# A hybrid decoder trunk on one core: another order of PE's and VectorE's work between the attention stage and the expert gathers

## What is computed

```python
x = x + (ga * ya + gb * yb) @ w_out                     # ya: state-space branch, yb: latent attention
x = x + peer(rmsnorm(x, norm_ffn), peer_wq, peer_keys, peer_u, peer_v)

def peer(h):                                            # 8 heads, 128 keys per half, top 16
    q = (h @ wq).reshape(blk, 8, 256)
    s1, s2 = q[..., :128] @ keys[:, 0], q[..., 128:] @ keys[:, 1]
    sc1, i1 = top_k(s1, 16); sc2, i2 = top_k(s2, 16)
    cand = sc1[..., :, None] + sc2[..., None, :]        # 16 x 16 sums
    sc, sel = top_k(cand, 16); idx = cidx[sel]          # 16 of 16,384 experts
    act = gelu(u[idx] . h)
    return sum(softmax(sc) * act * v[idx])
```

## Time and profile before

| | us |
|---|---|
| median of 3 runs | 2117.23 |
| lowest and highest | 2110.43, 2120.0 |
| the profiled execution | 2117.6 |
| its span | 2116.1 |
| PE busy in it | 1670.0 (79%) |
| VectorE busy | 1447.7 (68%) |
| ScalarE busy | 489.1 (23%) |
| bytes read | 735.70 MB |

### The profile page before, as it was taken

How to read it: one execution, slowest core, us unless ns; L and a number is a source line. 1 busy time by engine, 2 the same in 40 slices (tenths; PEclk the granted TensorE clock), 3 DMA queues, 4 the chain that set the end, 5 groups by cost and what they waited for, 6 DMA issues and landing times. The chain is left out here.

```text
span 2116.1 us, 30101 instructions
## 1 busy us (share of the span) xinstructions
PE 1670.0 (79%) x10874; PEld 842.1 (40%) x10874; DVE 1447.7 (68%) x3666; ACT 489.1 (23%) x1413; POOL 667.8 (32%) x614
## 2 busy tenths in 40 slices
PE   7999999877777666666789999997777866666666
PEld 6887677433333111111168786773332421111111
DVE  3557533778778878877726575347877878887786
ACT  2246211211121221111223553122121112111112
POOL 0011000444554454444300110004454444444442
PEclk9999999877897676665799999999787876666658
DMA  5458895999999999999854688969999999999997
GB/s 205 157 204 305 300 389 229 387 370 420 416 421 421 404 416 420 421 415 414 366 181 150 218 318 297 387 240 408 404 421 420 416 420 402 421 421 420 416 413 304
DMA packets 135936, 749.11 MB, mean 354 GB/s; under 512 B 16611, under 2 KB 17100, under 8 KB 57298
## 3 DMA queue, kind: packets, MB, share of 16 engines
q0 software_dynamic: 84640, 588.54, 68.2%
q1 hardware_dynamic: 51138, 158.55, 20.6%
HBM read 735.70 MB, written 11.52 MB: 353 GB/s over the span
## 5 line engine op out<-in xcount | busy, mean ns | idle before, releaser
L1221 PE MATMUL ps<-arena 64*64 64x512 f32 x4096 | 753.2, 836 | 384.0 <-DVE arena L1841 381.7
L2463 POOL DMA_INDIRECT arena<-in_peer_uv,arena x528 | 619.9, 1174 | 792.2 <-PE ps L1221 642.7
L1832 DVE CUSTOM_DVE_ANT_0 arena<-arena,h 128x1024 f32<-128x1024 f32 x512 | 627.3, 1225 | 241.3 <-DMA arena<-in_peer_uv,arena 235.4
L1221 PEld LDWEIGHTS ps<-arena 64*64 64x64 f32 x4096 | 141.1, 166 | 938.6 <-DVE arena L1841 889.7
L573 PE MATMUL ps<-ht_tok,wring 128*128 128x264 f32 (+1 forms) x1536 | 362.9, 395 | 4.5 <-DMA wring<-in_w_in 3.1
L2204 ACT ACTIVATE arena<-arena 128x1 f32<-128x1 f32 x528 | 105.4, 203 | 975.1 <-DVE arena L1832 974.0
L573 PEld LDWEIGHTS ps<-ht_tok,wring 128*128 128x128 f32 x1536 | 292.8, 194 | 75.6 <-issue 19.9
L1841 DVE TENSOR_SCALAR arena<-consts,arena 128x64 f32<-128x64 f32 (+1 forms) x528 | 164.6, 312 | 25.2 <-ACT arena L2204 24.6
L573 PE MATMUL ps<-arena,wring 128*128 128x264 f32 x256 | 64.1, 393 | 2.7 <-DVE arena L1536 2.7
L573 PE MATMUL ps<-arena,gate 128*128 128x256 f32 x256 | 59.0, 382 | 0.0
L2440 POOL DMA_DIRECT2D nrow<-in_norm_ffn x2 | 1.1, 536 | 174.2 <-PE ps L925 174.2
(11 more groups left out here) (374 smaller groups left out, 1791.3 us busy)
## 6 DMA issues: line engine op xcount, KB each, us to landing
arena<-in_pages SPq DMA_DIRECT2D x256, 272.0 KB, 6.1
wring<-in_w_in SPq DMA_DIRECT2D x36, 1024.0 KB, 5.0
arena<-in_peer_uv,arena POOLq DMA_INDIRECT x528, 12.8
h<-in_state_ssm POOLq DMA_DIRECT2D x16, 512.0 KB, 6.1
out<-h POOLq DMA_DIRECT2D x16, 512.0 KB, 6.3
wring<-in_w_ssm_proj SPq DMA_DIRECT2D x8, 1024.0 KB, 10.8
arena<-in_w_out SPq DMA_DIRECT2D x8, 1024.0 KB, 9.4
wring<-in_peer_wq SPq DMA_DIRECT2D x8, 1024.0 KB, 9.7
```

The lines of the kernel that those rows point to most:

```text
L1221: last = pe.matmul(ps[to:to + 64, SUM_BANK[t] + i, :], diag[rows, n % DIAGS, 0:64], ring[rows, HOME[n % RING], cols], start=n in TILE_FIRS ...
L1832: dve.tensor_tensor_reduce(ring[:, HOME[k], 0:D_MODEL], ring[:, HOME[k], 0:D_MODEL], tokens, 1.0, 0.0, ALU.mult, ALU.add, dots[:, column(n ...
L2463: pool.indirect_dma_start(ring[:, HOME[k], :], None, table, bass.IndirectOffsetOnAxis(ap=idx[:, TOPK * u + j:TOPK * u + j + 1], axis=0)).t ...
```

## The change

It moves the samples' attention output, heads and parts behind tile 0's output products and head 0's scores; sums tile 0's squares by quarters (three ahead of the last) and takes its rows by halves; sends the query weights of heads 0, 3, 4 and 2 at the end of the attention stage (head 2's into the gates' second half); searches heads 0 and 1 of tile 0 by eights, the first eight in the 8 x 8 corner of the sums (first_experts); puts head 1's queries and scores behind out(2,1) and ahead of the samples' sums and out(3,1); takes no step of head 1's search before slot 4 and four steps in each of slots 4 to 7; and moves the sums to x ahead of the dot product of slots 2 to 4, the rows of tiles 1 and 2 to slot 8, and PE's later turns and head 2's queries back by one slot. `lat_kept` is a copy of the samples' newest latents (ScalarE, behind the fifth half page). Turned rows are now contiguous slices; the host lays out peer_wq to match. In the arena the places of `diag` and `hot` move ahead.

```diff
     steps = {}
     for first in range(3):
-        steps[7 + first] = [("rows", first)]
+        steps[8 + first] = [("rows", first)]
     for hh in range(2, P_HEADS):
         begun = TOPK * (hh - 2) - (2 if hh == P_HEADS - 1 else 0)
-        at = (2, 6, 10) if hh > 2 else (11, 12, 14)
+        at = (2, 6, 10) if hh > 2 else (12, 13, 14)
         steps[begun + at[0]] = [("queries", hh, 0, 0, TOKENS)]
         steps[begun + at[1]] = [("queries", hh, 1, 0, TOKENS)]
         steps[begun + at[2]] = [("scores", hh, (0, 1))]
...
+        lat_kept = latroom[0:SAMPLES, DC * BLOCK:DC * BLOCK + KV_LORA]
...
+        wq_gates = gate[:, DC:, 0:BLOCK]
...
-            elif hh == 3:
-                pe.wait_ge(sem("early_load"), 16)
-                state["wq", hh] = wq_early
+            elif hh in (2, 3):
+                pe.wait_ge(sem("early_load"), 32)
+                state["wq", hh] = wq_early if hh == 3 else wq_gates
...
+        if (hh, m, lo) == (0, 0, 0):
+            for q in range(2):
+                pe.wait_ge(sem("aux_free"), 3 + q + marks["turned", 0])
+                last = product(ps[:, b, 0:P], lambda c: w[:, 4 * q + c, 0:P], lambda c: ht[:, 4 * q + c, 0:P], 4, start=q == 0, stop=q == 1)
+            wide.filled(last)
+        else:
+            wide.filled(product(ps[:, b, 0:hi - lo], lambda c: w[:, c, m * P:(m + 1) * P], lambda c: ht[:, c, lo:hi], DC))
...
     def scores(hh, tiles):
 
-        pe.wait_ge(sem("wide_free"), 4 + marks["q", hh])
         if (hh, tiles[0]) == (0, 0):
             pe.wait_ge(sem("keys_load"), 16)
+        else:
+            pe.wait_ge(sem("wide_free"), 4 + marks["q", hh])
         b = wide.fill()
         for t in tiles:
             for half in range(2):
+                if (hh, t) == (0, 0):
+                    pe.wait_ge(sem("wide_free"), 3 + half + marks["q", hh])
...
-    rows_of = lambda t, c: hp[t].rearrange("p (q c) -> p c q", c=DC)[:, c, :]
-
+    rows_of = lambda t, c: hp[t][:, c * P:(c + 1) * P]
...
+    def samples_mixed():
+
+        pe.wait_ge(sem("sample_mix"), 1)
+        pe.wait_ge(sem("lat_kept"), 1)
...
+    def first_rows(q):
+
+        pe.wait_ge(sem("ph_ready"), q + 1)
+        b = aux.fill()
+        for c in range(4 * q, 4 * q + 4):
+            last = turn(ps[:, b, (c % 4) * P:(c % 4 + 1) * P], rows_of(0, c), P)
+        aux.filled(last)
+        marks["turned", 0] = aux.n
+
+    marks["wq_block"] = state["n"]
+    pe.wait_ge(sem("mixed"), 1)
+    out(0, 0)
     pe.wait_ge(sem("half_sums"), 1)
     b = aux.fill()
     turn(ps[0:SAMPLES, b, 0:P], fin[:, 128:136], P)
     aux.filled(turn(ps[0:SAMPLES, b, P:2 * P], fin[:, 136:144], P))
-    marks["wq_block"] = state["n"]
-    pe.wait_ge(sem("mixed"), 1)
-    out(0, 0)
+    out(1, 0)
+    out(2, 0)
+    marks["x", 0] = aux.n
     pe.wait_ge(sem("sample_weights"), 1)
     b = aux.fill()
     aux.filled(turn(ps[:, b, 0:SAMPLES], fin[0:SAMPLES, 384:512], SAMPLES))
-    out(1, 0)
-    pe.wait_ge(sem("sample_mix"), 1)
...
-    out(2, 0)
-    pe.wait_ge(sem("wide_free"), 4 + marks["samples_mixed"])
...
     out(3, 0)
-    marks["x", 0] = aux.n
-    sample_heads()
-    sample_mla_parts()
-    pe.wait_ge(sem("ph_ready"), 1)
...
-    pe.wait_ge(sem("aux_free"), 4 + marks["turned", 0])
+    samples_mixed()
+    first_rows(0)
+    samples_turned()
+    first_rows(1)
     queries(0, 0, 0, P)
     queries(0, 1, 0, P)
     scores(0, (0,))
-    queries(1, 0, 0, P)
+    sample_heads()
+    sample_mla_parts()
+    out(0, 1)
     sample_mla()
-    queries(1, 1, 0, P)
-    out(0, 1)
-    scores(1, (0,))
     out(1, 1)
     pe.wait_ge(sem("mixed"), 2)
     out_samples(0)
     out_samples(1)
     out(2, 1)
+    queries(1, 0, 0, P)
+    queries(1, 1, 0, P)
+    scores(1, (0,))
     pe.wait_ge(sem("aux_free"), 4 + marks["sums"])
...
-    for k in range(1, 4):
-        out(k, 0)
-    px_mean(0, slice(45, 46))
+    dve.wait_ge(sem("px0_squares"), 1)
+    then(dve.tensor_reduce(st[:, 45:46], st[:, 54:57], AX.X, ALU.add))
+    dve.tensor_scalar(st[:, 45:46], st[:, 45:46], 1.0 / D_MODEL, EPS, ALU.mult, ALU.add).then_inc(sem("px0_squares_mean"), 1)
+    out(3, 0)
     dve.wait_ge(sem("ffn_row_load"), 16)
-    px_rows((0,))
+    dve.wait_ge(sem("px0_root"), 1)
+    then(dve.reciprocal(st[:, 51:52], st[:, 48:49]))
+    for q in range(2):
+        cols = slice(512 * q, 512 * q + 512)
...
+    def expert_numbers(u, k, width):
 
         eight = slice(8 * k, 8 * k + 8)
         split = lambda ap: ap.rearrange("p (s i) -> p s i", s=2)[:, :, eight]
-        dve.tensor_scalar(iw[:, 8 * k:8 * k + 8], ctopi[:, eight], 4, None, ALU.logical_shift_right)
-        then(dve.tensor_scalar(iw[:, TOPK + 8 * k:TOPK + 8 * k + 8], ctopi[:, eight], 15, None, ALU.bitwise_and))
+        dve.tensor_scalar(iw[:, 8 * k:8 * k + 8], ctopi[:, eight], {8: 3, TOPK: 4}[width], None, ALU.logical_shift_right)
+        then(dve.tensor_scalar(iw[:, TOPK + 8 * k:TOPK + 8 * k + 8], ctopi[:, eight], width - 1, None, ALU.bitwise_and))
         then(dve.tensor_copy(split(sel), split(iw)))
-        picks = hot[:, 256:512].rearrange("p (s i j) -> p s i j", s=2, j=TOPK)
-        then(dve.tensor_tensor(picks, bc(split(sel), 3, TOPK), bc(bc(cst("iota"), 1, 8), 1, 2), ALU.is_equal))
-        then(dve.tensor_tensor(picks, picks, bc(topf.rearrange("p (s j) -> p s j", s=2), 2, 8), ALU.mult))
+        yield
+        picks = hot[:, 256:256 + 16 * width].rearrange("p (s i j) -> p s i j", s=2, j=width)
+        then(dve.tensor_tensor(picks, bc(split(sel), 3, width), bc(bc(cst("iota")[:, 0:width], 1, 8), 1, 2), ALU.is_equal))
+        then(dve.tensor_tensor(picks, picks, bc(topf.rearrange("p (s j) -> p s j", s=2)[:, :, 0:width], 2, 8), ALU.mult))
+        yield
         then(dve.tensor_reduce(split(sel), picks, AX.X, ALU.add))
-        dve.scalar_tensor_tensor(out=idx[:, 8 * k:8 * k + 8], in0=sel[:, 8 * k:8 * k + 8], scalar=float(N_KEYS),
+        to = TOPK * u + 8 * k
+        dve.scalar_tensor_tensor(out=idx[:, to:to + 8], in0=sel[:, 8 * k:8 * k + 8], scalar=float(N_KEYS),
                                  in1=sel[:, TOPK + 8 * k:TOPK + 8 * k + 8], op0=ALU.mult, op1=ALU.add).then_inc(sem("idx_ready"), 1)
+        yield
+
+    def first_experts(u):
+
+        dve.wait_ge(sem("scores_out"), SCORES_AT[u, 0])
+        halves = [keysc[:, u, 0, half, :] for half in range(2)]
+        for k in range(2):
+            at = [slice(TOPK * half + 8 * k, TOPK * half + 8 * k + 8) for half in range(2)]
+            for half in range(2):
+                last = dve.max(top[:, at[half]], halves[half])
+            then(last)
+            yield
+            for half in range(2):
+                last = dve.max_index(topi[:, at[half]], top[:, at[half]], halves[half])
+            then(last)
+            yield
+            dve.tensor_scalar(topf[:, at[0]], topi[:, at[0]], layer_off[:, 1:2], None, ALU.add)
+            dve.tensor_copy(topf[:, at[1]], topi[:, at[1]])
+            width = 8 * (k + 1)
+            sums = cand[:, 0:width * width]
+            then(dve.tensor_tensor(sums.rearrange("p (i j) -> p i j", i=width), bc(top[:, 0:width], 2, width),
+                                   bc(top[:, TOPK:TOPK + width], 1, width), ALU.add))
+            yield
+            if k == 1:
+                then(dve.match_replace(sums, ctop[:, 0:8], sums, -3e38))
+                yield
+            eight = slice(8 * k, 8 * k + 8)
+            then(dve.max(ctop[:, eight], sums))
+            then(dve.max_index(ctopi[:, eight], ctop[:, eight], sums))
+            yield
+            yield from expert_numbers(u, k, width)
+            if k == 0:
+                for half in range(2):
+                    last = dve.match_replace(halves[half], top[:, at[half]], halves[half], -3e38)
+                then(last)
+                yield
+        w = wexp[:, TOPK * u:TOPK * u + TOPK]
+        dve.tensor_scalar(w, ctop, ctop[:, 0:1], None, ALU.subtract).then_inc(sem("experts_shifted"), 1)
...
-    for _ in best_experts(0):
+    for _ in first_experts(0):
         pass
+    out(0, 1)
     sample_gated()
-    out(0, 1)
-    ahead = best_experts(1)
-    for _ in range(10):
-        next(ahead)
     out(1, 1)
-    for half in range(2):
-        copy4(hp[2][:, half * 512:(half + 1) * 512])
-
-    def late_tiles(n):
-
-        if n == 1:
+    ahead = first_experts(1)
+
+    def early_tiles(n):
+
+        if n == 2:
+            for half in range(2):
+                copy4(hp[2][:, half * 512:(half + 1) * 512])
+        elif n == 3:
             out(2, 1)
-        elif n == 2:
+        elif n == 4:
             for half in range(2):
                 b = aux.read()
                 xs = x[0:SAMPLES, 2, half * 512:(half + 1) * 512]
                 aux.emptied(dve.tensor_tensor(xs, xs, ps[0:SAMPLES, b, :], ALU.add))
-        elif n == 3:
             out(3, 1)
-        elif n == 5:
+
+    def late_tiles(n):
+
+        if n == 7:
             px_mean(1, slice(46, 48))
-        elif n == 6:
+        elif n == 8:
             px_rows((1, 2))
...
```

(47 more changed lines are left out.)

96 lines of the change are left out of this document (48 added, 48 removed).

## The result

The changed kernel took 2142.35 us (median of 4 runs, 2136.27 to 2146.41), the kernel before 2118.61 (4 runs, 2110.43 to 2122.67): a ratio of **1.0115, 95% interval 1.008 to 1.015**. That is slower, by 24 us, and above the range that was forecast. The profiled execution took 2136.27 us, with a span of 2134.7 against 2116.1: 18.6 us more; it was the quickest of its four runs. The medians of the kernel before stood between 2115.6 and 2119.1 on the chips of the experiments, so ratios are compared rather than times.

The account below looks back on a forecast made before the run. DMA, filled by gathers of expert rows, was taken to bound the kernel. Gains of 0 (first layer), 1.2 (second) and 2.0 us (dips) sum to 3.2: 2117.6 - 3.2 gives 2114 us, range 2103 to 2127.

Parts of the forecast that it names:

- Bound: Each layer from about slot 10 of 264: DMA sets the pace, with 1 MB expert-row gathers every 2.5 us.
- place: Idle DMA between the last attention step and the saturated gathers: 45.7 us over both layers, all the change can touch.
- Earlier start: PE's chain behind "mixed", first layer: head 0's search starts at 355.2, not 362.9.
- corner search: VectorE's search for the first eight expert numbers: 3.7 us against 6.7; first gather at about 359.3, 10.6 us earlier.
- Early loads: Weights of heads 0, 3, 4, 2 and keys, 5 MB sent at 331.4 to 331.8: loaded by 346, before queries at 350.
- Head start: Less idle DMA around the first gathers: 5.7 us in the first layer, 4.1 us in the second.
- What follows: PE and VectorE behind head 0's scores, first layer: out(3,1) ends at 384.2, against 387.96; slot 9 at 404.5, before 401.8.
- Giving back: DMA gaps up to gather 23: 8.7 us in the first layer, nothing won; 3.3 in the second, 1.2 us won.
- the dips behind: Idle DMA around head 3's queries, 3.1 and 0.8 us: should shrink by about half, 2 us won.
- the clock rival: Slots 9 to 18: VectorE's pacing leaves PE at 1.2 GHz, 7.2 us price, 2131 us in all; chance 0.14.
- No gain: Gather 8 hangs on out(3,1), later ones on VectorE's slots 4 to 9; gain lost again, 2118 us; chance 0.20.
- Head start kept: Slots 4 to 9 go quicker than counted, DMA never runs dry: 11.7 us won, 2106 us; chance 0.24.

Follow-up runs that it names:

- experiment 1: Changed kernel with ScalarE taking head 1's query copies behind gelus 0 and 1 and the copy of the scores behind gelu 2: 2130.92 us, ratio 1.0085.
- experiment 4: Changed kernel with the loads of heads 5 and 6 sent only once head 1's first queries are done: 2132.02 us, ratio 1.0087.
- 5 both: Changed kernel with the edits of experiment 1 and experiment 4 together: 2129.53 us, ratio 1.0068.
- experiment 2: Changed kernel, head 1's queries, scores and copies earlier, eight of its search steps ahead of slot 0, sums to x in slots 1 to 3: 2123.27 us, ratio 1.0026.
- 3 two steps: Changed kernel with two steps of head 1's search a slot instead of four, reaching to slot 11: 2135.69 us, ratio 1.0082.
- 6 order, PE busy: Experiment 2 with two extra PE products, whose result nobody reads, behind the outputs of each of slots 3 to 7: 2115.78 us, ratio 0.9991.
- experiment 8: Experiment 2 with rows of tiles 1 and 2 in slot 6, not 8, and turns and head 2's queries a slot earlier: 2114.47 us, ratio 0.9976.
- 10 and later products: Experiment 8 with two extra PE products behind the outputs of slots 3 to 6 and 15 to 17: 2108.78 us, ratio 0.997.
- 12 and head 4's weights: The kernel of "10 and later products" with head 4's query weights sent ahead of "mixed" again: 2108.55 us, ratio 0.9951.
- experiment 7: The kernel before the change with two extra PE products behind the outputs of each of slots 3 to 6: 2116.81 us, ratio 0.9998.
- 9 and products in slots 3 to 6: Experiment 8 with two extra PE products behind the outputs of each of slots 3 to 6: 2110.41 us, ratio 0.9963.
- 11 changed, head 4's weights: Changed kernel with head 4's query weights sent ahead of "mixed" again, as before the change: 2139.7 us, ratio 1.0106.

## Why the prediction was wrong

**What held.** *Bound* and *place* held: DMA's idle time behind the last attention step is where most of the time was lost (13.7 of the 18.6 us between the profiled executions). *Earlier start* and *corner search* held to a microsecond: search from 354.65 (355.2 forecast), number written 3.9 us later (3.7), first gather at 358.79 (359.3), gather 6 at 373.90 (374.3). The MAX8 and FIND_INDEX8 of 64 took 0.23 and 0.22 us, inside the bounds taken. *Early loads* held for the five that go out at "mixed": head 0's queries start at 349.55 (350.3) without a wait for them. *Head start*: DMA had 7.2 us less idle time in the first 46 us of the first layer and 6.1 in the second, against 5.7 and 4.1 in the forecast. It also expected that the head start would be given back, but not that more than all of it would. One of its own signs of being wrong, out(3,1) ending after 388, came true by 0.2 us.

**The step that failed first** is in *What follows*: "so scores end at 378.8; sums 380.6, out(3,1) 384.2". They ended at 381.0, 384.1 and 388.2. The forecast had seen that ScalarE takes the copies only behind gelus 2 and 3, but let those dot products wait for out(2,1)'s sum alone. They waited for gather 3, and the forecast's own account gave its time: four gathers and three loads from 360.1 on are 17.5 us, so 377.6; it was summed only to ask when DMA would run dry. That is 2.2 of the 4.0 us by which out(3,1) was late; nearly all of the rest is the clock behind PE's wait (1.3 us in the sums, 0.4 in out(3,1)). Everything behind moved with it, by 4 to 5 us: slot 9 at 408.53 (404.5), the turns at 411.95 (407.9), head 2's queries at 424.25 (419.5). The second layer repeats it (gather 7 waits 12.57 us for PE, the sums take 2.97 us), so the loss is taken twice. Experiments 1, 4 and 5 show this wait: medians put it at 10 to 13 us of the 24, ratios at 6 to 10, with intervals that overlap the changed kernel's.

**The terms that were mis-sized** are those of *Giving back*. With out(3,1) at its forecast place (experiment 1) gather 23 still came at 101.1 and 101.5, against 98.1 and 91.9 before; the forecast had it equal in the first layer and 1.2 us won in the second. The two layers were not summed by one rule: the balance that gives 1.2 us for the second (head start less gaps, plus the idle time before) gives 5.7 - 8.7 + 0.5 = -2.5 us for the first, which was called nothing because gather 23 would end at 437.4 instead of "about 437.6", an end that no row shows. Measured in the changed kernel, the gaps from 46 to 106 us behind "mixed" are 11.0 and 10.4 us, against 8.7 and 3.3 in the forecast; the dips behind, which should have shrunk by 2 us in all, grew from 3.0 and 0.6 in the kernel before to 5.7 and 4.2.

The worst of it was the second layer, to which the forecast gave the clock of before, "back at full after slot 7". Before, the granted clock was 0.87 there in the window at 66 us; in the changed kernel it was 0.52, close to the 0.54 of the first layer. The change had left all 16 search steps to slots 4 to 7, where VectorE is busy for 18.1 of 20 us, and PE, paced by it, worked 12 to 13 of 20 us. This is the clock rival, given 0.14, for the reason it names ("with VectorE as the pacer that thin stretch grows"), though not at its size: head 2's queries took 4.58 us, not over 5. The Trainium skill (TensorE: Matmul & The Clock Gate, "HAM oscillation") describes matmuls that come in short bursts with waits for data between them and so start at the low clock each time. The traces agree from both sides, though each wait is short: in the window at 66 us the clock is 0.50 to 0.60 in experiments 1 to 5, 1.00 with the extra products. The price of the low clock, 7.4 us for both layers (experiments 2 and 6), is half of the 14 us that the rival named.

**The rivals.** *No gain* had the chain right (gather 8 and on hang on VectorE's slots 4 to 9) but bounded the loss at nothing. *Head start kept* needed the slots to go quicker; that takes the order of experiment 8, and its 2106 is near what experiments 10 and 12 reach (2108.8 and 2108.6 us), with fewer steps in the slots and the clock full, as it named. The forecast took the wait, the steps and the clock for independent small terms, and in the trace each feeds the next: behind the wait the clock is low, and the slots start later with all their steps still to do. How the 24 us divide among the three is not measured; the experiments' shares overlap.

**The yardstick.** Gather 23 marks the end of the stretch in which the kernels differ. Its start behind "mixed", summed over both layers, against the sum before (190.0), beside the difference of the medians:

| kernel | gather 23, both layers, less before | median less before |
|---|---|---|
| changed | +22.0 | +23.7 |
| 1 copies | +12.5 | +12.7 |
| 4 loads | +11.6 | +13.8 |
| 5 both | +10.7 | +13.9 |
| 3 two steps | +12.8 | +17.5 |
| 2 order | +4.9 | +5.0 |
| 6 order, PE busy | -1.6 | -3.3 |
| 7 before, PE busy | -4.0 | -2.3 |
| 8 order, rows | -6.3 | -4.6 |
| 9 and products in slots 3 to 6 | -6.3 | -8.7 |
| 10 and later products | -6.3 | -6.8 |
| 11 changed, head 4's weights | +21.9 | +21.8 |
| 12 and head 4's weights | -6.3 | -9.4 |

Over a range of some 30 us the two agree within 5 us; what happens behind gather 23, as in experiments 9, 10 and 12, it doesn't see. The first gather, which the forecast built its head start on, starts 28.0 us behind "mixed" in the changed kernel and in all those built on it, whose ratios go from 1.0115 to 0.9951: it says nothing about the time.

**What stays open.** 4.9 of the 18.6 us between the two profiled executions are in no DMA idle time that the windows show. They are busy time of DMA: summed over its packets, the 16 engines were busy for 1887.5 us of the span in the kernel before and for 1892.7 in the changed one, 5.2 us more for the same 749.16 MB. The same sum lies between 1882.9 and 1896.0 us over the 14 profiled executions of this study, so one profile against one can't say whether the change causes it; what makes the same bytes take longer stays open. Head 2's weights in 1 KB pieces are not it: the page's section 3 gives the queue of the direct loads 20.4% of 2134.7 us against 20.6% of 2116.1, 436 us both times, with 52,930 packets instead of 51,138. From 46 to 66 us behind "mixed", ahead of gather 7, which waits for out(3,1), DMA is idle for 1.3 us or more in every version with the early search but experiments 4 and 5, whose two late loads fill it (0.4 to 0.9 us); those loads were never tried together with the order of experiments 2 and 8.

## What to carry to other kernels

An earlier first transfer buys nothing while a chain of other engines releases the later ones; find the transfer at which the stretch ends and count back from that one. When loads are moved up against gathers, work out when each single gather lands, not only when the lot is through, and look at what stands behind its consumer in every in-order queue: here a copy behind a gelu on ScalarE stopped PE. Where PE is paced by another engine in short slots, give it real work there (turns, queries), or at least try useless products, before judging an order of work: here the clock was worth 7.4 us under experiment 2's order, and nothing measurable where DMA was full (experiment 7) or real work had already filled the slots (experiments 8 and 9).

## What the hardware showed that was not expected

Two useless products a slot (1.98 us) took the granted clock from 0.60 to 1.00 over 20 us and the ratio from 1.0026 to 0.9991. One engine's wait of 3.13 us was followed by products at a lower rate: 3.16 us for sums that take 1.88, and 4.10 for an output product of 3.73. A gather of 1 MB issued at 362.61 was used at 378.66, with three direct loads of 1 MB sent 4 to 5 us ahead of it; in experiment 4, with two of the three held back, this took 11.4 us instead of 16, and PE's wait behind it was gone.
